# Another order for the blocks, quarter products and down tiles of the gated stages

## The reference

```python
D_MODEL = 1024; SEQ = 256; DEPTH = 2; D_FF = 2816
def swiglu(h, w_gate_up, w_down):
    a, b = jnp.split(h @ w_gate_up, 2, axis=-1)
    return (jax.nn.silu(a) * b) @ w_down
...
x = x + 0.5 * swiglu(rms_norm(x, ffn1_norm), ffn1_w_gate_up, ffn1_w_down)
...
x = x + 0.5 * swiglu(rms_norm(x, ffn2_norm), ffn2_w_gate_up, ffn2_w_down)
```

## Time and profile before

| | us |
|---|---|
| median of 3 runs | 1408.11 (1407.59 to 1408.72) |
| the profiled execution, its own time | 1408.07 |
| its span, first to last instruction | 1406.3 |
| PE busy | 1399.9 (100%) |
| weight loads of PE (PEld) busy | 1196.1 (85%) |
| DVE busy | 1089.3 (77%) |
| ACT busy | 862.2 (61%) |
| POOL busy | 230.6 (16%) |
| a gated stage from N2 to d17, by windows | 153.96, one of 154.39 |

### The profile page before, as it was taken

How to read it: one execution, slowest core, us unless ns; L and a number is a source line. 1 busy time by engine, 2 the same in 40 slices (tenths; PEclk the granted TensorE clock), 3 DMA queues, 4 the chain that set the end, 5 groups by cost and what they waited for, 6 DMA issues and landing times.

```text
span 1406.3 us, 20191 instructions
## 1 busy us (share of the span) xinstructions
PE 1399.9 (100%) x7632; PEld 1196.1 (85%) x7632; DVE 1089.3 (77%) x1650; ACT 862.2 (61%) x1397; POOL 230.6 (16%) x307
## 2 busy tenths in 40 slices
PE   9999999999999999999999999999999999999999
PEld 7888888898888888888888888888888899888887
DVE  7878876776978878788775778788767877678776
ACT  6657656755667647576566646666567665455553
POOL 1112233000111001112050001114149200100000
PEclk9999999999999999999999999999999999999999
DMA  9999755464999859998564457999546445456651
GB/s 369 299 301 283 223 203 175 136 201 176 308 255 290 210 193 304 267 282 213 197 219 150 165 179 270 271 275 261 189 145 242 133 135 184 162 171 218 194 183 58
DMA packets 84049, 305.48 MB, mean 217 GB/s; under 512 B 9329, under 2 KB 9457, under 8 KB 83825
## 3 DMA queue, kind: packets, MB, share of 16 engines
q1 hardware_dynamic: 69840, 253.07, 51.0%
q0 software_dynamic: 13824, 50.34, 18.8%
q10 hardware_dynamic: 288, 0.79, 0.1%
HBM read 303.11 MB, written 1.05 MB: 216 GB/s over the span
## 4 chain that ended last, share of the span: by engine, by line
PE 98%; DVE 1%; DMA 0%; ACT 0%; issue 0%; POOL 0%; DVEq 0%; ACTq 0%; POOLq 0%
PE bank L733 18%; PE bank L740 9%; PE bank L687 9%; PE bank L688 9%; PE bank L689 9%; PE bank L893 5%; PE bank L892 5%; PE bank L896 5%; PE bank L754 4%; PE bank L759 4%; PE bank L755 4%; PE bank L717 3%; PE bank L724 3%; PE bank L718 3%; PE bank L707 1%; PE bank L992 1%
## 5 line engine op out<-in xcount | busy, mean ns | idle before, releaser
L1967 DVE TENSOR_TENSOR wlo<-raw,whi 128x1024 fp32r<-128x1024 f32 x409 | 492.3, 1231 | 12.3 <-ACT whi L1360 12.2
L1360 ACT ACTIVATE whi<-raw 128x1024 fp32r<-128x1024 f32 x409 | 417.5, 1048 | 17.1 <-PE bank L689 10.6
L733 PE MATMUL bank<-hx,whi 128*128 128x512 f32 x1088 | 268.6, 393 | 0.0
L733 PEld LDWEIGHTS bank<-hx,whi 128*128 128x128 f32 x1088 | 200.4, 188 | 41.3 <-issue 2.0
L687 PE MATMUL bank<-whi,hid 128*128 128x512 f32 x536 | 211.1, 394 | 0.0
L688 PE MATMUL bank<-wlo,hid 128*128 128x512 f32 x536 | 209.2, 390 | 0.0
L689 PE MATMUL bank<-whi,hid 128*128 128x512 f32 x536 | 208.8, 389 | 0.0
L740 PEld LDWEIGHTS bank<-hx,wlo 128*128 128x128 f32 x1088 | 142.9, 191 | 7.7
L740 PE MATMUL bank<-hx,wlo 128*128 128x256 f32 x1088 | 145.2, 282 | 0.0
L1967 DVE TENSOR_TENSOR wlo<-gates,whi 128x1024 fp32r<-128x1024 f32 x96 | 115.9, 1221 | 5.4 <-ACT whi L1360 5.0
L689 PEld LDWEIGHTS bank<-whi,hid 128*128 128x128 f32 x536 | 100.6, 188 | 21.4
(11 more groups left out here) (300 smaller groups left out, 2378.5 us busy)
## 6 DMA issues: line engine op xcount, KB each, us to landing
raw<-w_dram SPq DMA_DIRECT2D x414, 512.0 KB, 4.5
gates<-w_dram POOLq DMA_DIRECT2D x64, 512.0 KB, 8.0
gates<-w_dram SPq DMA_DIRECT2D x32, 512.0 KB, 5.7
arena<-w_dram POOLq DMA_DIRECT2D x32, 512.0 KB, 9.2
arena<-w_dram SPq DMA_DIRECT2D x16, 512.0 KB, 5.2
gain<-g_dram SPq DMA_DIRECT2D x7, 512.0 KB, 3.2
arena<-c_dram SPq DMA_DIRECT2D x2, 768.0 KB, 6.2
cst<-c_dram SPq DMA_DIRECT2D x1, 1056.0 KB, 7.5
```

Source lines behind the costliest of these rows:

```text
L733: e.matmul(b[:, :], hi_of(j)[:, k * P:k * P + P], hx[:, k * 2 * S:k * 2 * S + 2 * S], start=k == 0, stop=False, skip_group_check=True)
L1360: e.activation(hi_of(t), raw_of(t), ACT.Copy).then_inc(sem["w_hi"], 1)
L1967: e.tensor_tensor(lo_of(t), raw_of(t), hi_of(t).bitcast(F32), ALU.subtract).then_inc(sem["w_lo"], 1)
```

## The change

Only ORDER differs, the same words in another sequence; everything that is derived from it (plan, leads, banks, form loads) moves with it. d1 goes behind N3 and 2a directly behind d1 and x3; the first products of chunk a are one block sooner, h1 and y1 one block later; N6 goes ahead of 3b, 5a ahead of d5, N8 ahead of 4a; T0a goes ahead of 6b and 2b, T1a behind d8 and both, 3c behind T1a; 4b is ahead of 7c, and 7c, T0b, 1c, d12, 6c follow one another; T0c is ahead of d16 and d17, T1c last.

```diff
-ORDER = """N2 x0 x1 d0 d1 1a x2 x3 N3 d2 h0 y0 h1 y1 N4 3a d3 N5 2a 7a 3b d4 N6 6a d5 5a d6 N7 7b 4a N8 d7 1b 3c T0a d8 T1a 2b 6b
-           5b d9 d10 7c d11 4b d12 1c T0b 6c T1b 2c 5c d13 N17 4c d14 d15 d16 T0c T1c d17""".split()
+ORDER = """N2 x0 x1 d0 1a N3 d1 x2 x3 2a h0 y0 N4 h1 y1 3a d2 N5 d3 7a N6 3b d4 6a 5a d5 N7 7b N8 4a 1b d6 d7 T0a 6b 2b d8 T1a 3c
+           5b d9 d10 4b d11 7c T0b 1c d12 6c T1b 2c 5c d13 N17 4c d14 d15 T0c d16 d17 T1c""".split()
```

## The result

20 executions of each: before 1408.01 us (1407.55 to 1408.77), after 1410.66 us (1410.26 to 1414.73), ratio 1.0021, 95% interval 1.0015 to 1.0027. The median is 1.1 us above the forecast. Two of the 20 executions of the changed kernel took 1412.72 and 1414.73 us, at a mean granted clock of 0.999 and 0.998 where the other 18 have 1.000; neither was profiled.

What follows compares the result with a forecast made beforehand. PE was taken as the bound, busy nearly throughout, so reordering only removes or adds its waits. 1408.07 + 1.8 (T0c) + 0.2 (transposes) - 0.43 (L1f1) = 1409.6 us; range 1407.5 to 1415.0.

Steps and rivals of the forecast that it cites:

- T0c, +1.8 us: Before T0c: its multiplication ends 5.82 us after 4c, with only 5.44 us of cover; 0.45 us a stage, 1.8 in all.
- The transposes, +0.2: T0c and T1c separated: one more start behind a transpose, +0.04 us a stage, 0.2 in all.
- T1c's cover: Finish behind T1c, now last: its third hidden tile is covered by some 0.3 us, no cost.
- L1f1, -0.43: Stage L1f1: a slow DVE multiplication delayed T1b; the new order's 8 us of cover would absorb it, -0.43 us.
- 7c to 6c, nothing: 6c's weight form, added onto 7c's: landing may take up to 8.2 us, 7 us expected, so no cost.
- rival A: Adds for 6c land late, deciding from 8.2 us; 7.6 us lost at full price, 1417.2 us; chance 0.17.
- SP's queue, nothing: Start of stage: y1 slips 6 us, loads b6 and d4 queue behind; ACT up to 2 us late in N5, PE unaffected.
- y0 to 3a, T0a, N8, T0b: Short covers claimed to hold without cost: 0.9 us before 3a, 1.6 us for T0b's multiplication; T0a and N8 also covered.
- rival B: Another short cover fails, before 3a or at T0b's multiplication: 0.5 to 1 us a stage, 1411.6 to 1413.6; chance 0.15.
- C: Rival: the change does nothing, T0c's wait being hidden by a faster DVE chain; 1408.0 us; chance 0.15.
- D: Rival: faster, PE being below its peak in a way smoother supply mends; 1407.6 us at best; chance 0.03.

Runs made afterwards that it cites:

- experiment 11: Changed kernel with d16 again ahead of T0c, T1c ahead of d17, constants loaded at d3, and 5c moved behind d13: 1422.60 us, ratio 1.0104.
- experiment 3: Changed kernel with T0c one down tile sooner still, directly behind d14: 1424.04 us, ratio 1.0114.
- The tail alone: Kernel before with only the new end of the order, d14 d15 T0c d16 d17 T1c: 1410.01 us, ratio 1.0015.
- experiment 5: Kernel before with only the first part of the new order, up to 6a: 1410.09 us, ratio 1.0017.
- experiment 6: Kernel before with only 4b, 7c and T0b moved (4b d11 7c T0b 1c d12 6c): 1434.91 us, ratio 1.0197.
- experiment 10: Kernel before with only the new middle, from 5a on up to 4c d14: 1408.38 us, ratio 1.0004.
- experiment 7: Changed kernel with d12 moved behind 5c, so 6c, 2c and 5c come one down tile sooner: 1420.58 us, ratio 1.0090.
- experiment 4: Changed kernel with the load of constants and parameters moved from d8 to the first tile of 2b: 1411.13 us, ratio 1.0032.

## Why the forecast held, point by point

- **T0c, +1.8 us: right** to 0.02 us a stage. The chain of 4c's addition, SiLU and multiplication is the same 5.81 to 5.83 us in every kernel but that of experiment 11, where 4c itself waits for DVE, and experiment 3 shows it one for one with the distance, 3.15 us where 3.17 were due.
- **The transposes, +0.2: right in kind.** The tail alone cost 2.0 us, 1.7 of it the waits; the 0.3 left are the lone transposes and the finish behind T1c. T1c's cover held.
- **L1f1, -0.43: right in size, wrong in cause.** It was taken for a chance slip that the new cover would absorb. It was no chance, and nothing was absorbed: in the new order POOL's small operations do not meet the multiplication. That the number came true is luck.
- **7c to 6c, nothing: the step that failed,** a little. 7c's second add took 6.7 to 6.8 us in three stages, as reckoned, and 9.0 in L0f1, over the 8.2 allowed, yet no step waited for it there. But the sum stopped at the first pair: it named 1c's adds as "right behind them" and gave them no limit of their own. Of four adds within 3.4 us the fourth takes 11.1 to 13.1 us in the changed kernel, against a limit of about 12.5. Cost 0.56 us in the profiled L0f1, and 0.2 to 0.7 us in one or two stages of other runs. It is rival A's mechanism with the wrong pair, at a small part of its price.
- **SP's queue, nothing: right only by the place of the constants.** What the prediction said of y1, b6 and N5 held, but it did not follow the other thing that is tied to a tile's place, the load at d8. That load moved by 14 us. At its old time it costs 2 us beside the new first part (experiment 5), at its new time it costs the 0.6 us of L0f1.
- **y0 to 3a, T0a, N8, T0b: right.** The covers left are 1.22 us (3a), 2.35 (T0a) and 1.85 (T0b) in the changed kernel, and N7's second sum is done 1.6 us after N7's end, as forecast, 1.1 us ahead of N8's start; rival B did not come. **C** and **D** neither: the chain does not move, and no start of a matmul is quicker, in any kernel.
- **What is not explained:** the 0.4 us wait at L754 for ACT L1920 in stage M. It is in each kernel with both the new first part and the new middle, and absent where only one of them is new, but for the run of 4b alone, where it is 2.7 us. Nor why 1c's last add in L1f2 took 11.1 us in some executions and 12.7 to 12.9 in others. With these and L0f1 the sum of 1409.6 becomes 1410.6.

So the sign and the main term stood on a chain that could be read to the last 0.05 us, and of the 1.1 us that were missing 0.6 lay in a transfer and 0.4 in the wait of stage M, whose cause is open.

## What to carry to other kernels

When a step is moved toward the work that feeds it, count the chain from the trace and compare it with the distance in steps; it was good to 0.02 us here. Look which weight form each step needs and when its adds are issued: experiments 6 and 10 move 4b and 7c alike, and lost 27 and 0.6 us, the latter within its interval, as 6b's adds were issued late or soon. Give every transfer of a bunch its own limit, the last one above all, and look for loads that hang on the position of a tile and move with it. Look also at what stands behind a waiting instruction on its engine: in experiments 5, 6 and 7 the wait for a transfer was harmless in itself and an operation queued behind the waiting one was the loss.

## What the runs showed of the hardware

**Half clock after a pause.** PE fell to half clock (1.2 GHz; 0.50 to 0.53 granted over the stretches behind the pause) after a pause of 2.98 us in two stages of four in experiment 3, after 2.86 us in experiment 4, after 1.9 us in three of four in experiment 11, and after three of the four waits of 4b in experiment 6; a pause of 2.98 us in L0f1 of experiment 7 did nothing. Each time it cost some 1.4 to 2.9 us more. What decides it no run here shows. In the profile of the changed kernel, where PE's longest idle time is 1.0 us, the granted clock is 1.00 in all four stages.

**POOL beside DVE.** A DVE operation with two inputs and its output in SBUF took 2.73 us in place of 0.69 beside POOL's small operations in L1f1 and 0.99 in L1f2; in L0f1, where one of POOL's took 2.01 us, it kept its 0.69. Moved apart in L1f1 it is short. DVE's splits, which have two SBUF inputs too, took up to 1.35 us in place of 1.22 beside the same operations in the kernel before. Why this one multiplication was held so much longer is not shown, and POOL's own operations take anything from 0.25 to 3.2 us over the kernels, so its 2.01 us proves nothing. The Trainium skill, page GPSIMD Engine Reference (Specifications), says that GpSimd shares its SBUF interface with VectorE and that they contend where a VectorE instruction has two SBUF inputs; the trace agrees, by the 2.73 us and the 1.35.

**Adds from POOL in a bunch.** Alone a pair of 512 KB takes 5.3 and 6.8 us; issued within 3.4 us, four take 5.4, 6.7, 8.1 and 11.3 us (L1f1), and 7.7, 9.0, 11.7 and 13.1 us where the DMA engines are full with SP's loads.
